# Four units of seven products in gate-and-up blocks 1 to 7, a second set of sum buffers, and low parts of four plain chunks made by accumulating GpSimd transfers

## The chip, the cores and the metric

One core of one Trainium2 chip. The metric is the device time of one execution in microseconds. A measurement is the median of several executions.

## The reference, cut to what matters

One decoder layer over 272 tokens (16 meta tokens and 256 of the input) with a model width of 2048. First a token-mixing part, which the change does not touch. Then a SwiGLU feed-forward part on the 256 tokens, with a hidden width of 5632, all in float32:

```python
u = rmsnorm(h, pre_ffn_g[i])
ff = (jax.nn.silu(u @ w_gate[i]) * (u @ w_up[i])) @ w_down[i]
h = h + rmsnorm(ff, post_ffn_g[i])
```

## The kernel before, in words

**Chunks and the ring.** All weights stream through a ring of four slots (`WSLOTS = 4`). A chunk q is 128 partitions by 1024 float32 values, 512 KB. SyncE loads it into `raw[slot]`, in gate and up as two transfers of 256 KB: 512 columns of w_gate and the same 512 columns of w_up, for one tile kt of 128 input channels. ScalarE writes its rounded high part `w_hi[slot]` (`split_hi`, L554) once the chunk has landed and TensorE has used chunk q-4. VectorE writes the low part `w_lo = raw - w_hi` (`split_lo`, L907). SyncE loads chunk q+4 into the slot once `w_lo` of chunk q is made, and, where chunk q belongs to a unit of seven products, once all sums over its raw values are made as well (L442). SyncE issues its loads strictly in order.

**Products.** The tokens stand as the transposed tiles `uf` (a high and a low part), and a product of full precision is three matmuls: high by high, high by low, low by high (`three`, L1711 to L1713), each 128x128 by 512 columns. A block g of gate and up (g = 0 to 10) is 512 hidden columns, sixteen chunks, eight pairs of chunks. A plain pair (letter P) costs 2 chunks x 4 quarters x 3 = 24 matmuls. A pair under letter Z is done by a scheme with seven products instead of eight, 21 matmuls (`seven_products`): it needs four sums of the tokens' blocks (`sums_f`, made once, in block 0) and four sums of the weights' blocks, made anew for each pair. `ROUND` writes the order of the pairs of a block by hand: block 0 is `PPPPPPPP`, blocks 1 to 10 are `PPZPZPZP`.

**The weight sums.** `weight_sums` (VectorE, L1195 to L1204) makes one sum of 512 columns into `tx[0]`, then the low half of the first chunk (L1181), then `tx[1]` (L1200), then `tx[2:4]` together (L1204). ScalarE rounds them, two at a time, to `t_hi` (`weight_sums_hi`, L838), and VectorE makes `t_lo` (`weight_sums_lo`, L1211). In between VectorE makes the low part of the pair's second chunk. There is one set of buffers `tx`, `t_hi`, `t_lo` (the last lies over `tx`), and semaphore `t_used` tells that TensorE has read a sum. In a Z pair TensorE first multiplies with the chunks themselves (3, then 6 matmuls, and then both slots are free), and then with the sums (12 matmuls). It waits for `lo_done` of the second chunk after the first three.

**What else a block has.** Seven of the products of a block's Z pairs are collected in other banks than the plain ones and folded in afterwards: in the next block's chunk 1 ScalarE copies one bank (`x0_kept`, L888) and VectorE makes combinations (`fold_sums`, L1265 to L1272); in its chunk 3, when TensorE has used every chunk of the block, VectorE folds them into the quarters (L1278, L1282), ScalarE applies silu (L815, after its `w_hi` of chunk 3) and VectorE multiplies gate and up (`gated`, L1169). TensorE transposes the result before its chunk 2 (L1774); in chunk 5 ScalarE and VectorE split it into `ffn` (L819, L1174). The order of each engine's work is the order of these loops, chunk by chunk; each engine is in order. In block 0 VectorE also makes `sums_f` for the three pairs of `SEVEN_F`, at the chunks in `F_SUM_AT`.

GpSimd has no work in this part.

Of the kernel before, what the change touches and what calls it, by code (L numbers as in the profile page):

```python
# [18 lines left out]
F32 = mybir.dt.float32  # L19
# [17 lines left out]
def build_trunk(nc, x, meta, pre_mix_g, w_in, w_pool, pool_scale, w_dw, b_dw, conv_ln_g, conv_ln_b, w_pw,  # L37
# [123 lines left out]
    with ExitStack() as ctx:  # L161
# [29 lines left out]
        t_lo = sb_at("t_lo", [P, 4, DCOLS], F32R, a_xt)  # L191
        t_hi = sb_at("t_hi", [P, 4, DCOLS], F32R, a_xt + 16 * DCOLS)
        rows_u = tx[:, 0, :].rearrange("p (k t) -> p k t", k=2)
        sums_w = tx[:, 1, :].rearrange("p (s t) -> p s t", s=4)
# [3 lines left out]
        sums_f = sb_at("sums_f", [P, len(SEVEN_F), 4, 2, P], F32R, a_y)  # L198
        gated = sb_at("gated", [P, NQ, DCOLS], F32, a_y + 4 * KT * SEQ - 8 * DCOLS)
        sums_y = sb_at("sums_y", [P, max(len(SEVEN_U) - IN_U, 1), 3, 2, P], F32R, a_y)  # L200
        assert 32 * P * len(SEVEN_F) + 8 * DCOLS <= 4 * KT * SEQ and 24 * P * (len(SEVEN_U) - IN_U) <= 4 * KT * SEQ
# [108 lines left out]
        def sem(name):  # L310
# [87 lines left out]
        def _(sp_eng):  # L398
# [64 lines left out]
        def _(pool):  # L463
# [85 lines left out]
        def _(act):  # L549
            def split_hi(q, slot, turn):  # L550
                act.wait_ge(raw_landed[slot], landed(q))
                if not isinstance(q, int) or q >= WSLOTS:
                    act.wait_ge(chunks_used, q - WSLOTS + 1)
                act.activation(w_hi[:, slot, :], raw[:, slot, :], ACT.Copy).then_inc(hi_done, 1)  # L554

            def split(q):
                split_hi(q, q % WSLOTS, q // WSLOTS)
# [346 lines left out]
        def _(dve):  # L904
# [279 lines left out]
            def weight_sums(q, z):  # L1184

                at = [(q - 1) % WSLOTS, q % WSLOTS]
                b11, b12, b22 = (raw[:, at[k], j * DCOLS:(j + 1) * DCOLS] for k, j in ((0, 0), (0, 1), (1, 1)))
                for k in range(2):
                    dve.wait_ge(raw_landed[at[k]], landed(q - 1 + k))
                if z == 0:  # L1190
                    dve.wait_ge(s_lo, 2 * len(SEVEN_F))
                else:
                    dve.wait_ge(t_used, 4 * z - 3)
                    dve.wait_ge(fold_done, len(QUARTERS) * max(min(SEVENS[z][0], NFG) - 1, 0))
                dve.tensor_tensor(tx[:, 0, :], b12, b11, ALU.add).then_inc(t_made, 1)  # L1195
                first_half_lo(q - 1)
                if z:
                    dve.wait_ge(t_used, 4 * z - 2)
                dve.wait_ge(t_made, 3 * z + 1)
                dve.tensor_tensor(tx[:, 1, :], b22, tx[:, 0, :], ALU.subtract).then_inc(t_made, 1)  # L1200
                if z:
                    dve.wait_ge(t_used, 4 * z)
                dve.wait_ge(t_made, 3 * z + 2)
                dve.tensor_tensor(tx[:, 2:4, :], raw[:, at[0]:at[0] + 2, 0:DCOLS],  # L1204
                                  tx[:, 1:2, :].to_broadcast([P, 2, DCOLS]), ALU.add).then_inc(t_made, 1)

            def weight_sums_lo(z):
                dve.wait_ge(t_made, 3 * z + 3)
                for h in range(2):
                    dve.wait_ge(t_hi_done, 2 * z + h + 1)  # L1210
                    dve.tensor_tensor(t_lo[:, 2 * h:2 * h + 2, :], tx[:, 2 * h:2 * h + 2, :],  # L1211
                                      hi_view(t_hi[:, 2 * h:2 * h + 2, :]), ALU.subtract).then_inc(t_lo_done, 1)

# [81 lines left out]
            for q in range(Q_FFN + 10, END + 4):  # L1295
                if q < END:
                    g, ch, d = place_of(q)
                    z = SEVEN_NO.get((g, d))
                    if 1 <= g <= NFG and ch == 3:
                        dve.wait_ge(chunks_used, BEGIN[g])  # L1300
                        inner_product(g - 1)
                    if z is None:
                        split(q)
                    elif ch % 2:
                        weight_sums(q, z)
                        split(q)
                        weight_sums_lo(z)
# [57 lines left out]
        def _(pe):  # L1365
# [357 lines left out]
            def plain_products(q, quarters):  # L1723
                g, ch, d = place_of(q)
                kt, chs = 2 * d + ch % 2, 2 * len(ROUND[g])
                pe.wait_ge(lo_done, q + 1)
                if g >= NFG:
                    pe.wait_ge(f_lo, kt // 4 + 1)
                for m, j in quarters:
                    if g == 0:  # L1730
# [4 lines left out]
            def seven_products(q):  # L1735
# [110 lines left out]
```

## Time and profile before

| | |
|---|---|
| time, median of 3 runs | 1076.89 us (1075.95 to 1077.07) |
| the profiled execution: its own time | 1076.7 us |
| its span | 1074.8 us |
| granted TensorE clock, mean of the span | 0.998 |

The profile is of one execution. Its rows are in microseconds from the span's start, unless they say ns. A row of the timeline gives the start, the length, the engine, the line of the kernel, the operation, output<-input, and how long the engine sat idle before it and what ended that. Neighbouring instructions of one engine overlap a little at their ends, so the distance of two starts is less than the length shown. Matmuls overlap far more: each row is about 0.39 us long, though the next begins 0.23 us after it.

### The profile page before, as it was taken

The numbers are of one execution on the slowest core, as the hardware profiler recorded it, in microseconds if no ns is written. First come the engines' busy times: TensorE is split into PE (matmuls) and PEld (weight loads), VectorE is DVE, ScalarE is ACT, GpSimd is POOL, SyncE is SP. The second block draws the span as 40 slices with busy tenths as digits, with TensorE's granted clock in tenths as the row PEclk, the third lists the DMA queues.
The fourth block names the chain that finished last, engine by engine and source line by source line (L and its number), as shares of the span: only waits on it lengthen the run. The fifth ranks groups of instructions, "written<-read, shape, count | busy, mean of one in ns | idle before, by whom it ended". The sixth has DMA issues, their size and how long they took to land. (4 is left out here: it accounts for less than half of the span.)

```text
span 1074.8 us, 15382 instructions
## 1 busy us (share of the span) xinstructions
PE 1064.1 (99%) x5745; PEld 922.1 (86%) x5745; DVE 891.3 (83%) x1083; ACT 599.2 (56%) x736; POOL 27.3 (3%) x46
## 2 busy tenths in 40 slices
PE   9999999999999999999999999999999999999996
PEld 8999999999888888888888888888888888888885
DVE  5699987646646787898998998988989899988887
ACT  6554454736545565555565655655655555655553
POOL 4000101101000000000000000000000000000000
PEclk9999999999999999999999999999999999999999
DMA  8655535444386476766756656657667655566665
GB/s 273 208 176 167 172 106 160 136 143 138 111 309 213 141 263 186 225 188 191 225 174 195 216 182 210 201 178 229 186 190 219 226 197 196 194 209 219 200 202 191
DMA packets 113208, 208.06 MB, mean 194 GB/s; under 512 B 9184, under 2 KB 46496, under 8 KB 111856
## 3 DMA queue, kind: packets, MB, share of 16 engines
q1 hardware_dynamic: 111952, 201.49, 58.6%
q10 hardware_dynamic: 608, 4.20, 1.0%
q0 software_dynamic: 576, 1.40, 0.4%
q8 instruction: 46, 0.75, 0.3%
q14 instruction: 26, 0.21, 0.1%
HBM read 202.86 MB, written 4.19 MB: 193 GB/s over the span
## 5 line engine op out<-in xcount | busy, mean ns | idle before, releaser
L554 ACT ACTIVATE w_hi<-raw 128x1024 fp32r<-128x1024 f32 x322 | 337.9, 1059 | 260.4 <-PE ps L1713 149.6
L907 DVE TENSOR_TENSOR w_lo<-raw,w_hi 128x1024 fp32r<-128x1024 f32 x322 | 390.4, 1226 | 82.5 <-ACT w_hi L554 81.9
L1711 PE MATMUL ps<-w_hi,uf 128*128 128x512 f32 x524 | 205.3, 392 | 0.1
L1713 PE MATMUL ps<-w_hi,uf 128*128 128x512 f32 x524 | 204.1, 389 | 0.0
L1712 PE MATMUL ps<-w_lo,uf 128*128 128x512 f32 x524 | 203.9, 389 | 0.0
L1375 PE MATMUL ps<-u,w_hi 128*128 128x272 f32 (+1 forms) x544 | 158.8, 292 | 0.0
L1377 PE MATMUL ps<-u,w_hi 128*128 128x272 f32 (+1 forms) x544 | 155.9, 287 | 0.0
L1378 PE MATMUL ps<-u,w_lo 128*128 128x272 f32 (+1 forms) x544 | 155.7, 286 | 0.0
L838 ACT CAST t_hi<-tx 128x1024 fp32r<-128x1024 f32 x92 | 96.3, 1052 | 65.9 <-DVE tx L1200 54.6
L1713 PEld LDWEIGHTS ps<-w_hi,uf 128*128 128x128 f32 x524 | 98.4, 188 | 20.6
L1711 PEld LDWEIGHTS ps<-w_hi,uf 128*128 128x128 f32 x524 | 98.4, 188 | 20.5 <-issue 0.5
L1712 PEld LDWEIGHTS ps<-w_lo,uf 128*128 128x128 f32 x524 | 98.4, 188 | 20.0
L1211 DVE TENSOR_TENSOR t_lo<-tx,t_hi 128x1024 fp32r<-128x1024 f32 x92 | 108.2, 1218 | 0.0
L1375 PEld LDWEIGHTS ps<-u,w_hi 128*128 128x128 f32 x544 | 102.4, 188 | 0.4
L1377 PEld LDWEIGHTS ps<-u,w_hi 128*128 128x128 f32 x544 | 102.5, 188 | 0.2
L1378 PEld LDWEIGHTS ps<-u,w_lo 128*128 128x128 f32 x544 | 102.6, 189 | 0.0
L1711 PE MATMUL ps<-w_hi,ffn 128*128 128x512 f32 x256 | 99.7, 389 | 0.0
L1713 PE MATMUL ps<-w_hi,ffn 128*128 128x512 f32 x256 | 99.6, 389 | 0.0
L1712 PE MATMUL ps<-w_lo,ffn 128*128 128x512 f32 x256 | 99.6, 389 | 0.0
L1204 DVE TENSOR_TENSOR tx<-raw,tx 128x1024 f32<-128x1024 f32 x46 | 56.4, 1225 | 4.7
L1711 PEld LDWEIGHTS ps<-w_hi,ffn 128*128 128x128 f32 x256 | 48.1, 188 | 10.0
L1712 PEld LDWEIGHTS ps<-w_lo,ffn 128*128 128x128 f32 x256 | 48.1, 188 | 10.0
(271 smaller groups left out, 1469.7 us busy)
## 6 DMA issues: line engine op xcount, KB each, us to landing
raw<-in_w_gate SPq DMA_DIRECT2D x176, 256.0 KB, 2.9
raw<-in_w_up SPq DMA_DIRECT2D x176, 256.0 KB, 3.5
raw<-in_w_down SPq DMA_DIRECT2D x88, 512.0 KB, 4.2
raw<-in_w_in SPq DMA_DIRECT2D x72, 512.0 KB, 3.6
raw<-in_w_out SPq DMA_DIRECT2D x32, 512.0 KB, 4.4
arena<-in_x SPq DMA_DIRECT2D x2, 1024.0 KB, 5.9
arena<-in_x ACTq DMA_DIRECT2D x2, 1024.0 KB, 8.5
out<-h2rows SPq DMA_DIRECT2D x2, 1024.0 KB, 5.5
```

The lines of the kernel that those rows point to most:

```text
L554: act.activation(w_hi[:, slot, :], raw[:, slot, :], ACT.Copy).then_inc(hi_done, 1)
L838: act.copy(t_hi[:, 2 * h:2 * h + 2, :], tx[:, 2 * h:2 * h + 2, :]).then_inc(t_hi_done, 1)
L907: dve.tensor_tensor(w_lo[:, slot, :], raw[:, slot, :], hi_view(w_hi[:, slot, :]), ALU.subtract).then_inc(lo_done, 1)
L1204: dve.tensor_tensor(tx[:, 2:4, :], raw[:, at[0]:at[0] + 2, 0:DCOLS], tx[:, 1:2, :].to_broadcast([P, 2, DCOLS]), ALU.add).then_inc(t_made, 1)
L1211: dve.tensor_tensor(t_lo[:, 2 * h:2 * h + 2, :], tx[:, 2 * h:2 * h + 2, :], hi_view(t_hi[:, 2 * h:2 * h + 2, :]), ALU.subtract).then_inc(t ...
L1375: pe.matmul(outs[m], w_hi[:, slot, at], x_hi, start=start and not (one_bank and m), stop=False, skip_group_check=True)
L1377: pe.matmul(outs[m], w_hi[:, slot, at], x_lo, start=False, stop=False, skip_group_check=True)
L1378: mm = pe.matmul(outs[m], w_lo[:, slot, at], x_hi, start=False, stop=last and k == len(kts) - 1, skip_group_check=True)
L1711: pe.matmul(o, a[0], b[0], start=start, stop=False)
L1712: pe.matmul(o, a[0], b[1], start=False, stop=False)
L1713: return pe.matmul(o, a[1], b[0], start=False, stop=stop)
```

## The change

In blocks 1 to 7 the order of pairs becomes `PPZZPZZP`, with four Z pairs; blocks 8 to 10 keep three. A fourth pair of token sums is made in block 0. In these blocks the Z pairs alternate between the old set of sum buffers and a second one, which lies in a part of `ffn` that is written from block 8 on (`gated` moves there too). For chunks 1, 2, 8 and 15 of these blocks VectorE no longer makes `w_lo`: ScalarE writes minus the high part into `w_lo` with one more pass over the raw chunk, right after its high part, and GpSimd issues a transfer that adds `raw` onto it in SBUF. TensorE does the eight matmuls of such a chunk that need the high part alone first, then waits for the transfer, then does the four with the low part. SyncE's load of chunk q+4 waits for the transfer as well.

```diff
-    SEVEN_F, SEVEN_U = (0, 1, 2), (11, 12, 13, 14, 15, 16, 17, 18, 19)
+    SEVEN_F, SEVEN_U = (0, 1, 2, 3), (11, 12, 13, 14, 15, 16, 17, 18, 19)
...
-    F_SUM_AT = {10: 0, 12: 1, 14: 2}
-    ROUND = ["PPPPPPPP"] + ["PPZPZPZP"] * (NFG - 1) + ["PPPPZPPZPPZPPZPZPZPZPP", "PPPZPZPZPZPZPZPZPZPZPP"]
+    F_SUM_AT = {10: 0, 12: 1, 13: 2, 14: 3}
+    WITH_SPARE = range(1, 8)
+    ADDED_CH = (1, 2, 8, 15)
+    ROUND = ["PPPPPPPP"] + ["PPZZPZZP" if g in WITH_SPARE else "PPZPZPZP" for g in range(1, NFG)] + ["PPPPZPPZPPZPPZPZPZPZPP", "PPPZPZPZPZPZPZPZPZPZPP"]
...
+    ADDED = [BEGIN[g] + ch for g in WITH_SPARE for ch in ADDED_CH]
+    ADDED_NO = {q: i for i, q in enumerate(ADDED)}
...
+    def buffers_of(z):
+
+        g, d = SEVENS[z]
+        return (z - SEVENS_TO[g - 1]) % 2 if g in WITH_SPARE else 0
...
-                sp_eng.wait_ge(lo_done, q - WSLOTS + 1)
+                if q - WSLOTS in ADDED_NO:
+                    sp_eng.wait_ge(lo_added[q % WSLOTS], lo_by_dma(q - WSLOTS))
+                else:
+                    sp_eng.wait_ge(lo_done, lo_by_dve(q - WSLOTS))
...
+            for i, q in enumerate(ADDED):
+                slot = q % WSLOTS
+                pool.wait_ge(neg_done, i + 1)
+                pool.dma_start(w_lo[:, slot, :].bitcast(F32), raw[:, slot, :], accum_op=ALU.add).then_inc(lo_added[slot], 16)
...
+            def minus_hi(q):
+                slot = q % WSLOTS
+                act.activation(w_lo[:, slot, :], raw[:, slot, :], ACT.Copy, scale=-1.0).then_inc(neg_done, 1)
...
                         split(q)
+                        if q in ADDED_NO:
+                            minus_hi(q)
                         if z is not None:
                             weight_sums_hi(z)
...
-                    if z is None:
+                    if z is None and q not in ADDED_NO:
                         split(q)
...
+                if q in ADDED_NO:
+                    pe.wait_ge(hi_done, q + 1)
+                    for m, j in quarters:
+                        for h in range(2):
+                            pe.matmul(quarter(g, m, j), left(g, kt, m)[h], right(q, j)[0], start=ch == 0 and h == 0, stop=False)
+                    pe.wait_ge(lo_added[q % WSLOTS], lo_by_dma(q))
+                    for m, j in quarters:
+                        mm = pe.matmul(quarter(g, m, j), left(g, kt, m)[0], right(q, j)[1], start=False, stop=ch == chs - 1)
+                    return mm
```

`lo_by_dve(q)` and `lo_by_dma(q)` count the low parts that each of the two makers has finished. In `weight_sums` the waits for `t_used` now name the Z pair that last used the same set of buffers.

## Rows read from the trace of the kernel before

**Rows 1.** Page, part 1: busy us (share), x instructions; then all PE waits over 0.1 us

```profile
PE 1064.1 (99%) x5745; PEld 922.1 (86%) x5745; DVE 891.3 (83%) x1083; ACT 599.2 (56%) x736; POOL 27.3 (3%) x46
...
PE ps L1417 <- POOL cst L467: 1.2, 1, 1.2
PE ps L1485 <- DVE u L928: 0.5, 1, 0.5
```

**Rows 2.** Busy time by engine in one block, 455.00 to 497.40

```profile
core 0: us, PE busy (x) PEld busy (x) DVE busy (x) ACT busy (x) POOL busy (x), PEclk, DMA share, GB/s
455.00:497.40 42.40, 42.40 (x193) 35.18 (x192) 38.59 (x40) 24.11 (x26) 0.00 (x0) 1.00 0.64 199
```

**Rows 3.** Timeline, TensorE, block 2: transposes, chunk 2, unit of seven, next pair

```profile
460.41 1.04 PE L1774 MATMUL ps<-cst,gated 128*128 128x128 f32 x8
...
461.98 0.40 PE L1711 MATMUL ps<-w_hi,uf 128*128 128x512 f32 x1
...
468.13 0.39 PE L1711 MATMUL ps<-w_hi,sums_f 128*128 128x512 f32 x1
...
471.53 0.39 PE L1711 MATMUL ps<-w_hi,uf 128*128 128x512 f32 x1
```

**Rows 4.** Timeline, VectorE, same block and `gated` of the next

```profile
457.89 1.41 DVE L1169 SCALAR_TENSOR_TENSOR gated<-ps,cst,gated 128x512 f32<-128x512 f32 x2 [0.20 <-DVE ps L1282]
...
468.03 2.35 DVE L907 TENSOR_TENSOR w_lo<-raw,w_hi 128x1024 fp32r<-128x1024 f32 x2
470.29 0.68 DVE L1195 TENSOR_TENSOR tx<-raw 128x512 f32<-128x512 f32 x1
...
472.29 1.23 DVE L1204 TENSOR_TENSOR tx<-raw,tx 128x1024 f32<-128x1024 f32 x1
473.43 1.22 DVE L907 TENSOR_TENSOR w_lo<-raw,w_hi 128x1024 fp32r<-128x1024 f32 x1
...
476.84 1.22 DVE L907 TENSOR_TENSOR w_lo<-raw,w_hi 128x1024 fp32r<-128x1024 f32 x1
...
500.30 1.41 DVE L1169 SCALAR_TENSOR_TENSOR gated<-ps,cst,gated 128x512 f32<-128x512 f32 x2 [0.20 <-DVE ps L1282]
```

**Rows 5.** Timeline, ScalarE, same block

```profile
456.19 1.25 ACT L815 ACTIVATE gated<-ps,cst 128x512 f32<-128x512 f32 x2
...
473.55 1.05 ACT L838 CAST t_hi<-tx 128x1024 fp32r<-128x1024 f32 x1 [0.28 <-DVE tx L1204]
474.51 1.06 ACT L554 ACTIVATE w_hi<-raw 128x1024 fp32r<-128x1024 f32 x1
```

**Rows 6.** DMA issues: KB each, median us from issue to landing

```profile
raw<-in_w_up SPq DMA_DIRECT2D x176, 256.0 KB, 3.5
...
out<-f_acc SPq DMA_DIRECT2D x3, 512.0 KB, 2.7
side<-in_w_pw POOLq DMA_DIRECT2D x1, 1024.0 KB, 7.7
...
side<-in_w_pool POOLq DMA_DIRECT2D x1, 256.0 KB, 4.4
```

**Rows 7.** Timeline, GpSimd: issue of the 256 KB; then DMA queues, 10 to 22

```profile
11.58 1.21 POOL L505 DMA_DIRECT2D side<-in_w_pool  x1
...
DMA  9999999999999999997478999999999995487996
```

**Rows 8.** Timeline, SyncE's queue, two loads of one block

```profile
473.59 0.33 SPq L445 DMA_DIRECT2D raw<-in_w_gate  x1
...
475.05 0.43 SPq L445 DMA_DIRECT2D raw<-in_w_up  x1
```

**Rows 9.** Timeline, VectorE, end of block 0: low parts and the idle time before them

```profile
408.50 1.23 DVE L907 TENSOR_TENSOR w_lo<-raw,w_hi 128x1024 fp32r<-128x1024 f32 x1 [1.12 <-ACT w_hi L554]
411.22 1.23 DVE L907 TENSOR_TENSOR w_lo<-raw,w_hi 128x1024 fp32r<-128x1024 f32 x1 [1.49 <-ACT w_hi L554]
416.00 1.41 DVE L1169 SCALAR_TENSOR_TENSOR gated<-ps,cst,gated 128x512 f32<-128x512 f32 x2 [3.55 <-ACT gated L815]
```

More of the change, by code:

```diff
@@ L153, in place_of, with lo_by_dve, lo_by_dma, before_in_buffers @@
         return g, ch, TURNS[g][ch // 2]
+    ADDED = [BEGIN[g] + ch for g in WITH_SPARE for ch in ADDED_CH]
+    ADDED_NO = {q: i for i, q in enumerate(ADDED)}
+    def lo_by_dve(q):
+        return q + 1 - sum(1 for a in ADDED if a <= q)
+    def lo_by_dma(q):
+        return 16 * sum(1 for a in ADDED if a <= q and (a - q) % WSLOTS == 0)
+    def buffers_of(z):
+        g, d = SEVENS[z]
+        return (z - SEVENS_TO[g - 1]) % 2 if g in WITH_SPARE else 0
+    def before_in_buffers(z):
+        return max((y for y in range(z) if buffers_of(y) == buffers_of(z)), default=None)
     def landed(q):
@@ L192, in build_trunk @@
         t_hi = sb_at("t_hi", [P, 4, DCOLS], F32R, a_xt + 16 * DCOLS)
+        a_spare = top[0] + 4 * KT * SEQ + 4 * 1152 + 4 * 4 * (max(WITH_SPARE) + 1) * 2 * SEQ
+        tx2 = sb_at("tx2", [P, 4, DCOLS], F32, a_spare)
+        t_lo2 = sb_at("t_lo2", [P, 4, DCOLS], F32R, a_spare)
+        t_hi2 = sb_at("t_hi2", [P, 4, DCOLS], F32R, a_spare + 16 * DCOLS)
+        sums_of, hi_of, lo_of = (tx, tx2), (t_hi, t_hi2), (t_lo, t_lo2)
         rows_u = tx[:, 0, :].rearrange("p (k t) -> p k t", k=2)
@@ L198, in build_trunk @@
         sums_f = sb_at("sums_f", [P, len(SEVEN_F), 4, 2, P], F32R, a_y)
[L199 removed]
+        gated = sb_at("gated", [P, NQ, DCOLS], F32, a_spare + 32 * DCOLS)
         sums_y = sb_at("sums_y", [P, max(len(SEVEN_U) - IN_U, 1), 3, 2, P], F32R, a_y)
[L201 removed]
+        assert 32 * P * len(SEVEN_F) <= 4 * KT * SEQ and 24 * P * (len(SEVEN_U) - IN_U) <= 4 * KT * SEQ
         side = sb_at("side", [P, KT * SEQ], F32, a_y)
@@ L206, in build_trunk @@
         a_ff = place(4 * FT * 2 * SEQ)
+        assert a_spare == a_ff + 4 * 32 * 2 * SEQ and 32 * DCOLS + 8 * DCOLS <= 4 * 12 * 2 * SEQ
         ffn = sb_at("ffn", [P, FT, 2, SEQ], F32R, a_ff)
@@ L347, in build_trunk @@
             sem(n) for n in ("rows_done", "turned", "h2_hi", "h2_lo", "h2_sq", "r2c_done"))
+        neg_done, lo_added = sem("neg_done"), [sem(f"lo_added{s}") for s in range(WSLOTS)]
         silu_done, p_done, f_hi, f_lo = (sem(n) for n in ("silu_done", "p_done", "f_hi", "f_lo"))
@@ L1189, in weight_sums @@
                     dve.wait_ge(raw_landed[at[k]], landed(q - 1 + k))
+                sums, y = sums_of[buffers_of(z)], before_in_buffers(z)
                 if z == 0:
                     dve.wait_ge(s_lo, 2 * len(SEVEN_F))
-                else:
-                    dve.wait_ge(t_used, 4 * z - 3)
+                if y is not None:
+                    dve.wait_ge(t_used, 4 * y + 1)
+                if y is not None and buffers_of(z) == 0:
                     dve.wait_ge(fold_done, len(QUARTERS) * max(min(SEVENS[z][0], NFG) - 1, 0))
-                dve.tensor_tensor(tx[:, 0, :], b12, b11, ALU.add).then_inc(t_made, 1)
+                dve.tensor_tensor(sums[:, 0, :], b12, b11, ALU.add).then_inc(t_made, 1)
                 first_half_lo(q - 1)
-                if z:
-                    dve.wait_ge(t_used, 4 * z - 2)
+                if y is not None:
+                    dve.wait_ge(t_used, 4 * y + 2)
                 dve.wait_ge(t_made, 3 * z + 1)
-                dve.tensor_tensor(tx[:, 1, :], b22, tx[:, 0, :], ALU.subtract).then_inc(t_made, 1)
-                if z:
-                    dve.wait_ge(t_used, 4 * z)
+                dve.tensor_tensor(sums[:, 1, :], b22, sums[:, 0, :], ALU.subtract).then_inc(t_made, 1)
+                if y is not None:
+                    dve.wait_ge(t_used, 4 * y + 4)
                 dve.wait_ge(t_made, 3 * z + 2)
-                dve.tensor_tensor(tx[:, 2:4, :], raw[:, at[0]:at[0] + 2, 0:DCOLS],
-                                  tx[:, 1:2, :].to_broadcast([P, 2, DCOLS]), ALU.add).then_inc(t_made, 1)
+                dve.tensor_tensor(sums[:, 2:4, :], raw[:, at[0]:at[0] + 2, 0:DCOLS],
+                                  sums[:, 1:2, :].to_broadcast([P, 2, DCOLS]), ALU.add).then_inc(t_made, 1)
             def weight_sums_lo(z):
+                b = buffers_of(z)
                 dve.wait_ge(t_made, 3 * z + 3)
@@ L1301, in _ @@
                         inner_product(g - 1)
-                    if z is None:
+                    if z is None and q not in ADDED_NO:
                         split(q)
-                    elif ch % 2:
+                    elif z is not None and ch % 2:
                         weight_sums(q, z)
```

15 lines of the change are left out of this document (8 added, 7 removed).

## The prediction

> **What bounds the kernel now.** I read the page's busy shares and TensorE's waits first: TensorE is busy for 99% of the span and waited 1.2 us once and 0.5 us once, never in gate and up [rows 1]. So fewer matmuls are time, as long as nothing makes TensorE wait. Then one block: from one `gated` to the next is 500.30 - 457.89 = 42.41 us [rows 4], in which VectorE is busy for 38.59, ScalarE for 24.11, GpSimd never, and the DMA engines for 0.64 [rows 2]. VectorE is the engine with no room, so what matters next is when each of its results is due.
>
> **Clock of a block.** Between two plain products 42 matmuls apart lie 471.53 - 461.98 = 9.55 us, 0.227 us each; the transposes put chunk 2 back by about 0.9 us (they start at 460.41, and the matmul at 461.98 is the fourth of that chunk, so the first stands for 461.30) [rows 3]. Chunks 0 and 1 are 24 matmuls, 5.44 us, so the block begins at 460.41 - 5.44 = 454.97; I call this 0. Check: 183 matmuls x 0.2268 + 0.9 = 42.4.
>
> **The gain.** A fourth Z pair takes 24 - 21 = 3 matmuls out of a block: 0.68 us. In seven blocks 21 matmuls, 4.8 us, if nothing waits.
>
> **VectorE's load.** A Z pair costs it 476.84 - 470.29 = 6.55 us, two low parts 470.29 - 468.03 = 2.26 [rows 4]. A fourth Z adds 4.3, four low parts less take off 4.5: even. ScalarE gets, per block, four more passes of about 1 us and one more Z (two sums of 1.05, and a half pass for a whole one): some 6 us on 24 of 42; room as a sum, but it is in order.
>
> **Where results are late: the second Z of a row.** VectorE's second Z in a row (pair 3) takes the place of the low parts at 468.03, so all of that unit moves 2.26 us earlier. Its second chunk's low part, which ended at 473.43 + 1.22 = 474.65, ends at 472.39. TensorE wants it three matmuls after pair 3 begins: 471.53 + 0.68 = 472.21. With the handoff I price this stall at 0.3 us; the sums behind it are just in time. Nothing earlier can help, because VectorE's `inner_product` starts only when the block before is used up. The same place at pair 6 has its slack back, as TensorE has a plain pair before both.
>
> **Where results are late: chunk 8.** ScalarE cannot touch chunk 8 before it has rounded the sums of pair 3. Its row at 473.55 moves to 471.29, the high part at 474.51 to 472.25 [rows 5], the new pass minus-high follows 0.96 later and ends at 474.27, which is 19.3. TensorE begins pair 4 at 471.53 + 21 x 0.227 = 476.29 and, after eight matmuls with the high part, wants the low part at 478.1. So the transfer, from GpSimd's wait to its landing, has about 4 us. Call it L. After it come 4 + 12 + 21 + 21 + 24 = 82 matmuls, 18.6 us, to the block's end. With 0.1 for handoffs a block takes 38.0 + L, or 42.0 (41.7 by the matmuls and 0.3) where L is under 4. Break-even with 42.4 is at L = 4.4. Chunks 1, 2 and 15 by the same working have over 5 us.
>
> **What L is.** No row shows an accumulating transfer, nor one from SBUF to SBUF. Nearest are two transfers that GpSimd issued: 256 KB landed after 4.4 us and 1024 KB after 7.7 [rows 6], 1.2 us of it the issue, in a stretch with the DMA engines 99% busy [rows 7]; between them 512 KB is 5.5. From below: 512 KB out of SBUF on SyncE's queue took 2.7 [rows 6], and with 1.2 for the issue 3.9. From above: the adding reads its destination too. Reading 512 KB more at (7.7 - 4.4)/768 us per KB gives 5.5 + 2.2 = 7.7. A quieter stretch takes off, a second read puts on; I take 5.2, near the one row pair that went through the same issuer, and keep 3.9 to 7.7 for the range. The Trainium skill, "Collectives: The Full Stack", on why ReduceScatter is half of AllGather, says that an add in the DMA engines needs two source reads and halves the rate; no row here shows it. By the block's own rate it would make a sum of L that is 0.64 x 42.4/16 = 1.7 us longer than a copy's.
>
> **What late adding does next.** SyncE's load of the next block's chunk 3 waits for chunk 15's transfer, and ScalarE's silu stands behind the high part of that chunk 3. Pair 6 needs chunks 12 and 13, which load behind chunk 8's transfer: a landing is 3.5 [rows 6], the second chunk's issue about 0.8 behind [rows 8], so VectorE begins pair 6 at 19.3 + L + 4.3; the last sums are rounded and ScalarE is at chunk 14 4.2 us later (470.29 to 474.51 [rows 4, 5]), three passes more end at 30.8 + L, the transfer at 30.8 + 2L, the load at 34.3 + 2L. That is L - 3.7 after the next block's start; a high part (1.06, overlapping) and the first silu (half of 1.25) [rows 5] end at L - 2.0, while `gated` starts at 2.9 today [rows 4]. So above L = 4.9 each us is paid a second time: at 5.2 it is 0.3. Block time 38.0 + 5.2 + 0.3 = 43.5, +1.1 us, in seven blocks +7.7.
>
> **At nothing.** The fourth token sum (about 2.4 us of VectorE) falls in the end of block 0, where VectorE idles 1.12, 1.49 and 3.55 us waiting for ScalarE [rows 9]; without that cover it would cost its 2.4 once. The second buffer set removes the `t_used` waits between neighbouring Z pairs; `gated`'s new place has no user before block 8. GpSimd's queue holds nothing else here, so what waits behind an add is only the next add. Stages outside blocks 1 to 7 stay.
>
> **Sum.** The profiled execution is 1076.7 us, its span 1074.8; the median is 1076.9, 0.2 above. 1076.9 + 7.7 = 1084.6.
>
> **Rivals.** (a) *The add is quick, the change pays.* L of 4.1 or less, near the lower bound: 41.7 + 0.3 = 42.0 per block, -0.4 x 7 = -3, 1073.9; for it: a plain SBUF read of this size takes 2.7, and the engines are a third idle; against it: both GpSimd rows are over 4.4. The Trainium skill, "DMA: Bandwidth & Descriptors", in the anatomy of a DMA on the GpSimd path, fits 2.0 us plus bytes/436e3: 3.2 us for 512 KB, which would bring this case about; its 4.4 for 1 MB stands against this trace's 7.7, so the trace does not agree, though in a crowded stretch. Chance 0.25. (b) *Even.* L of 4.1 to 4.7: gain and stalls cancel, 1075 to 1079. Chance 0.18. (c) *Chunk 8 is late*, the forecast: L of 4.7 to 6.5, that is +0.3 to +3.7 per block, 1079 to 1103. Chance 0.44. (d) *The DMA engines become the bound.* 512 KB costs the sixteen engines 1.7 us by the block's rate; four adds are 7 us as copies and 14 with a second read, on top of 27 of 42: a share of 0.80 to 0.96, loads land late, L is 7 to 8: 38 + 7 + 2.1 = 47.1, +33 us or more, 1110 to 1124. For it: 0.64 today [rows 2]; against it: the gaps between loads are long. Chance 0.13.
>
> **How the numbers follow.** About 0.2% (2.2 us) is what a measurement of this kernel can tell. Faster is (a), 0.25 (38.0 + 4.1 is 0.3 per block under today's 42.4); same is (b), 0.18; slower is (c) and (d), 0.57. The range runs from (a) at 1073.3 to L = 6.5 at 1103, leaving out (d) and a little below. The forecast's own range is 1079 to 1103.
>
> **What would show it.** 21 matmuls less, 28 + 7 = 35 whole low parts fewer at VectorE's L907 (a Z pair has a half for one of its two), 28 transfers on GpSimd's queue. Right: TensorE rows with idle time ended by a DMA on `w_lo`, in chunk 8 of each block, of 1 to 2 us; small idle times at pair 3 ended by VectorE's L907; loads of chunk 12 issued later. A landing time of the adding transfers under 4.1 makes the forecast wrong at that step; waits of TensorE at chunks 1, 2 or 15, or at `w_hi`, would make it wrong in place.

## The result, and the profile after

The changed kernel takes 1131.44 us (median of 5 runs, 1129.66 to 1132.93), 54.5 us more than the 1076.89 before: ratio 1.0509, 95% interval 1.0497 to 1.0521. The forecast had the sign, but 7.7 us; the measured time lies far above its range.

The page of the changed kernel: busy times; the granted clock and DMA share in 40 slices; two of its queues.

```profile
PE 1073.4 (95%) x5724; PEld 914.9 (81%) x5724; DVE 891.2 (79%) x1096; ACT 634.4 (56%) x779; POOL 51.4 (5%) x74
...
PEclk9999999999999999999999999999999999999999
DMA  8655454424685776867768676776675656566665
...
q1 hardware_dynamic: 111952, 201.49, 55.6%
q0 software_dynamic: 4608, 16.08, 7.2%
```

The matmuls went from 5745 to 5724, the 21 promised; VectorE's work is the same (891.2 against 891.3 [rows 1]), and ScalarE, with its 35 us more, is busy for the same 56%. The granted clock is at the upper level, 2.4 GHz, in all of blocks 1 to 7 but one stretch: behind TensorE's wait of 2.48 us for `gated` it fell, to a mean of 0.57 from 520 to 524, so mostly to the lower level, 1.2 GHz. Over the 49.8 us from 517.4 to 567.2 the mean is 0.97. As an estimate, the length times what the mean lacks to 1.00 is what the clock cost, 1.5 us here; I use this estimate below as well. So the loss is waiting, nearly all of it. From one `gated` to the next, the kernel before took 41.9 to 42.8 us. In the changed kernel the seven intervals that belong to blocks 1 to 7 take 50.9, 51.3, 49.8, 51.6, 49.2, 50.8 and 49.5 us, and the blocks after them 41.6, 42.4 and 42.4 again. So the loss is 8 us a block.

One block, 460.40 to 510.85 (length, busy times by engine, granted clock, DMA share, GB/s, as in [rows 2]), and then the largest waits that the change made or enlarged (total us, times, longest; the first three rows are of ScalarE and VectorE, the others of TensorE):

```profile
460.40:510.85 50.45, 43.67 (x190) 34.07 (x189) 38.31 (x41) 29.13 (x33) 3.41 (x4) 1.00 0.74 209
```

```profile
ACT w_hi L590 <- DMA raw<-in_w_up: 92.9, 50, 3.7
...
DVE tx L1240 <- issue: 28.1, 15, 2.6
...
DVE gated L1212 <- ACT gated L855: 25.7, 8, 6.4
...
PE ps L1757 <- DVE w_lo L950: 17.5, 16, 1.7
...
PE ps L1781 <- DMA w_lo<-raw: 11.4, 14, 1.3
...
PE ps L1829 <- DVE gated L1212: 10.5, 6, 2.5
...
PE ps L1757 <- DVE ffn L1217: 6.3, 6, 1.1
```

```profile
SPq L477 <- DMA w_lo<-raw: 124.9, 28, 6.7
```

Where [rows 2] had TensorE busy for all of the block, it is now idle for 6.8 of 50.45 us, and VectorE, the engine that had no room, idles 12. (Most of what 6.8 leaves of the loss stands in TensorE's busy time, 43.67 us for 190 matmuls where 193 took 42.40: a matmul's row is 0.39 us long though the next begins after 0.23, and the row behind a wait is longer.) TensorE's waits in blocks 1 to 7 are 17.5 us for VectorE's low parts (L950), 11.4 for the transfers (L1781), 10.5 for `gated` and 6.3 that end with VectorE's `ffn`. So the transfers themselves are a quarter of them; the rest is VectorE being late. The largest row is ScalarE waiting for raw chunks to land, 92.9 us against 18.9 in the kernel before. SyncE's queue waits for the adding transfers 28 times, 124.9 us in all. Its total wait at that line is what it was before (117.8 and 124.9 now, 243.7 then); what is new is when the loads go. The transfers and the loads:

```profile
raw<-in_w_gate SPq DMA_DIRECT2D x176, 256.0 KB, 3.5
raw<-in_w_up SPq DMA_DIRECT2D x176, 256.0 KB, 4.1
...
w_lo<-raw POOLq DMA_DIRECT2D x28, 512.0 KB, 6.2
```

```profile
DMA to landing us min/median/max: 5.0/6.2/7.8
```

L, from issue to landing, was 6.2 us where I took 5.2 between 3.9 and 7.7 [rows 6]; the issue is 0.86 of it. The loads' medians are 3.5 and 4.1 us, 0.6 more than the 2.9 and 3.5 before. Here is one held load after another (timelines of GpSimd, SyncE's queue, ScalarE and VectorE around the start of the block that begins at 460.4):

```profile
453.00 0.85 POOL L575 DMA_DIRECT2D w_lo<-raw  x1 [18.09 <-ACT w_lo L594]
457.08 0.85 POOL L575 DMA_DIRECT2D w_lo<-raw  x1 [3.23 <-ACT w_lo L594]
```

```profile
459.29 0.33 SPq L477 DMA_DIRECT2D raw<-in_w_gate  x1
...
463.60 1.58 SPq L477 DMA_DIRECT2D raw<-in_w_up  x1
```

```profile
464.49 1.06 ACT L590 ACTIVATE w_hi<-raw 128x1024 fp32r<-128x1024 f32 x1 [2.74 <-DMA raw<-in_w_up]
465.45 1.25 ACT L855 ACTIVATE gated<-ps,cst 128x512 f32<-128x512 f32 x2
```

```profile
466.15 1.41 DVE L1212 SCALAR_TENSOR_TENSOR gated<-ps,cst,gated 128x512 f32<-128x512 f32 x2 [3.08 <-ACT gated L855]
...
470.36 0.69 DVE L1240 TENSOR_TENSOR tx<-raw 128x512 f32<-128x512 f32 x1 [1.66 <-issue]
```

Chunk 15's transfer, issued at 453.00, lets the load of the next chunk 3 go at 459.29; that chunk is rounded at 464.49, silu follows and `gated` starts at 466.15, 5.7 us into the block instead of 2.9. Chunk 1's transfer, issued at 457.08, lets the load of chunk 5 go, its second half at 463.60; it lands at 470.3, and only then can VectorE begin the sums of pair 2, at 10.0 us into the block instead of 5.4, as this row of the kernel before shows:

```profile
460.35 0.69 DVE L1195 TENSOR_TENSOR tx<-raw 128x512 f32<-128x512 f32 x1
```

Everything behind it is late by that: chunk 8's transfer is issued at 24.1 us into the block, where I had 19.3.

The first of the seven blocks shows what a held load does by itself, as no transfer of an earlier block disturbs its start. TensorE's transposes of blocks 1 and 2, and VectorE's first sum of pair 2 in block 1, in the changed kernel:

```profile
417.29 1.04 PE L1829 MATMUL ps<-cst,gated 128*128 128x128 f32 x8
...
467.62 1.09 PE L1829 MATMUL ps<-cst,gated 128*128 128x128 f32 x8 [1.63 <-DVE gated L1212]
```

```profile
420.02 0.69 DVE L1240 TENSOR_TENSOR tx<-raw 128x512 f32<-128x512 f32 x1 [2.25 <-issue]
```

Block 1 begins 5.44 us before its transposes, at 411.85, so the sum begins at 8.2 us into the block; in the kernel before it is 5.9 (418.46, with the transposes at 418.04). The load of chunk 5 had gone out at 416.18, when chunk 1's transfer, issued at 409.79, was done. And from transposes to transposes this first block takes 50.3 us already, the next one 51.3.

### The profile page after: what moved, and what is told of

It is laid out like the page before. It is cut to its first block and busy times, and to the rows that moved or that the text cites. A ratio compares the mean times of both kernels' runs of the same rounds, so it can differ in the third digit from the quotient of the medians.

```text
span 1129.4 us, 15468 instructions
## 1 busy us (share of the span) xinstructions
PE 1073.4 (95%) x5724; PEld 914.9 (81%) x5724; DVE 891.2 (79%) x1096; ACT 634.4 (56%) x779; POOL 51.4 (5%) x74
## 5 line engine op out<-in xcount | busy, mean ns | idle before, releaser
L590 ACT ACTIVATE w_hi<-raw 128x1024 fp32r<-128x1024 f32 x315 | 330.0, 1058 | 259.7 <-DMA raw<-in_w_up 92.9
L950 DVE TENSOR_TENSOR w_lo<-raw,w_hi 128x1024 fp32r<-128x1024 f32 x287 | 349.5, 1226 | 80.8 <-ACT w_hi L590 80.2
L1757 PE MATMUL ps<-w_hi,uf 128*128 128x512 f32 x370 | 146.9, 397 | 17.7 <-DVE w_lo L950 17.5
L879 ACT CAST t_hi<-tx 128x1024 fp32r<-128x1024 f32 x106 | 110.8, 1050 | 81.3 <-DVE tx L1245 67.7
L1759 PE MATMUL ps<-w_hi,uf 128*128 128x512 f32 x370 | 144.3, 390 | 0.0
L1758 PE MATMUL ps<-w_lo,uf 128*128 128x512 f32 x370 | 144.2, 390 | 0.0
L1257 DVE TENSOR_TENSOR t_lo<-tx,t_hi 128x1024 fp32r<-128x1024 f32 x106 | 124.7, 1218 | 0.0
L1757 PEld LDWEIGHTS ps<-w_hi,uf 128*128 128x128 f32 x370 | 69.4, 188 | 39.9 <-DVE w_lo L950 25.1
L1759 PEld LDWEIGHTS ps<-w_hi,uf 128*128 128x128 f32 x370 | 69.5, 188 | 14.7
L1758 PEld LDWEIGHTS ps<-w_lo,uf 128*128 128x128 f32 x370 | 69.5, 188 | 13.6
L1249 DVE TENSOR_TENSOR tx<-raw,tx 128x1024 f32<-128x1024 f32 x53 | 64.9, 1225 | 5.8 <-DVE tx L1245 0.5
L1240 DVE TENSOR_TENSOR tx<-raw 128x512 f32<-128x512 f32 x53 | 36.5, 688 | 38.3 <-issue 28.1
L1778 PE MATMUL ps<-w_hi,uf 128*128 128x512 f32 x224 | 57.4, 399 | 0.0
```

Of the source, the lines that this page charges most:

```text
L879: act.copy(hi_of[b][:, 2 * h:2 * h + 2, :], sums_of[b][:, 2 * h:2 * h + 2, :]).then_inc(t_hi_done, 1)
L950: dve.tensor_tensor(w_lo[:, slot, :], raw[:, slot, :], hi_view(w_hi[:, slot, :]), ALU.subtract).then_inc(lo_done, 1)
L1249: dve.tensor_tensor(sums[:, 2:4, :], raw[:, at[0]:at[0] + 2, 0:DCOLS], sums[:, 1:2, :].to_broadcast([P, 2, DCOLS]), ALU.add).then_inc(t_ma ...
L1257: dve.tensor_tensor(lo_of[b][:, 2 * h:2 * h + 2, :], sums_of[b][:, 2 * h:2 * h + 2, :], hi_view(hi_of[b][:, 2 * h:2 * h + 2, :]), ALU.subt ...
L1757: pe.matmul(o, a[0], b[0], start=start, stop=False)
L1758: pe.matmul(o, a[0], b[1], start=False, stop=False)
```

## The experiments

Each is a change of the changed kernel, and its blocks are told by the distance from one `gated` to the next (kernel before: 42.4). In the fences of experiments the line numbers are of their own kernels. The first question was what the seven neighbouring pairs cost without any transfer.

**Four units of seven, no transfers.**

```diff
-    ADDED_CH = (1, 2, 8, 15)
+    ADDED_CH = ()
```

> Four units of seven in blocks 1 to 7 with both sets of sum buffers, but no transfers: VectorE makes all low parts. Theory A (the adding transfers hold the ring: SyncE's load of chunk q+4 waits for the transfer of chunk q, and such waits chain through a block): most of the 54.5 us go; what is left is VectorE's own excess, 38.6 + 4.3 = 42.9 us of work and some 2 us of gaps against 41.7 of matmuls, +1 to +3.5 us per block, 1084 to 1101. Rival B (the neighbouring units of seven are too late by themselves, transfers or not): 1120 or more.

1085.17 us, ratio 1.0084 (1.0067 to 1.0101); blocks 43.3 to 44.1. TensorE has two waits per block, at pairs 3 and 6:

```profile
517.33 0.50 PE L1757 MATMUL ps<-w_hi,uf 128*128 128x512 f32 x1 [0.61 <-DVE w_lo L950]
532.96 0.50 PE L1757 MATMUL ps<-w_hi,uf 128*128 128x512 f32 x1 [0.33 <-DVE w_lo L950]
```

So the transfers cost 46 of the 54.5 us, and the pairs themselves about 9. Rival B falls.

**The transfers with the old order of pairs.**

```diff
-    SEVEN_F, SEVEN_U = (0, 1, 2, 3), ...
+    SEVEN_F, SEVEN_U = (0, 1, 2), ...
-    F_SUM_AT = {10: 0, 12: 1, 13: 2, 14: 3}
+    F_SUM_AT = {10: 0, 12: 1, 14: 2}
-    ADDED_CH = (1, 2, 8, 15)
+    ADDED_CH = (1, 2, 10, 15)
-    ... ["PPZZPZZP" if g in WITH_SPARE else "PPZPZPZP" for g in range(1, NFG)] ...
+    ... ["PPZPZPZP"] * (NFG - 1) ...
```

> The order of pairs, the token sums and the number of units of seven as in the kernel before; chunks 1, 2, 10 and 15 of blocks 1 to 7 have their low parts added by transfers, and VectorE has 4.5 us less to do per block. Theory A: the chained waits are there though VectorE has room, 3 to 7 us per block, 1098 to 1126. Rival B: with room on VectorE nothing is late, 1075 to 1082.

1103.91 us, ratio 1.0259 (1.0241 to 1.0276), blocks 44.0 to 49.5. TensorE hardly waits for a low part here (1.1 us in all), yet the kernel loses 27 us:

```profile
ACT w_hi L590 <- DMA raw<-in_w_up: 85.4, 46, 7.9
...
PE ps L1829 <- DVE gated L1212: 12.8, 6, 4.3
...
PE ps L1781 <- DMA w_lo<-raw: 1.1, 3, 0.4
```

The transfers do harm even where VectorE has 4.5 us of room more, and they landed in 5.3 us at the median here, nearly the 5.2 that I had forecast. ScalarE's long waits for raw chunks point at late loads. A small part is the clock's: behind two waits of 4.1 and 4.3 us for `gated` the granted clock was 0.93 and 0.96 over the block, by my estimate 5 us in all.

**Adding from HBM, so that raw is free earlier.**

```diff
-                    sp_eng.wait_ge(lo_added[q % WSLOTS], lo_by_dma(q - WSLOTS))
+                    sp_eng.wait_ge(neg_done, ADDED_NO[q - WSLOTS] + 1)
...
-                pool.dma_start(w_lo[:, slot, :].bitcast(F32), raw[:, slot, :], accum_op=ALU.add).then_inc(lo_added[slot], 16)
+                g, ch, d = place_of(q)
+                for j, src in enumerate((wg_v, wu_v)):
+                    pool.dma_start(w_lo[:, slot, j * DCOLS:(j + 1) * DCOLS], src[:, 2 * d + ch % 2, g * DCOLS:(g + 1) * DCOLS], accum_op=ALU.add).then_inc(lo_added[slot], 16)
```

> As the changed kernel, but the adding transfer reads the weights from HBM again (two of 256 KB per chunk), so raw is free once ScalarE has made both of its passes, and SyncE waits for that instead of the transfer. Theory A: the chain between transfer and load is cut, only TensorE's own waits for the low parts of chunk 8 and its like stay: +1 to +4 us per block, 1085 to 1105. Rival C (the transfers slow the loads by sharing the sixteen engines; who waits for them does not matter): the HBM traffic rises further, 1125 or more.

1147.67 us, ratio 1.0654 (1.0637 to 1.0672), a miss of theory A's range; it lies in rival C's. ScalarE's waits for raw did fall (26.7 us instead of 92.9), and the loads landed in 3.6 and 4.4 us, about as in the changed kernel (3.6 and 4.3), so what rival C names is not seen. But the second of the two transfers landed after 9.0 us and TensorE waited for it 45.3 us; behind such waits the granted clock fell, to 0.91 over three of the seven blocks and 0.97 over the other four, by my estimate 21 us in all. Held slots were exchanged for longer transfers, so this run tells nothing apart.

**A copying transfer.** The low parts of the four chunks are raw values here.

```diff
-                pool.dma_start(w_lo[:, slot, :].bitcast(F32), raw[:, slot, :], accum_op=ALU.add)...
+                pool.dma_start(w_lo[:, slot, :].bitcast(F32), raw[:, slot, :])...
```

> As the changed kernel, but the transfer copies raw onto the low part instead of adding it (the low parts are then wrong by the high part). If the second read of the add is what makes it long, the landing falls from 6.2 us to about 4.5 and the time to 1095 to 1115; if the path of issue and descriptors is, the landing stays near 6 and the time within 8 us of 1131.

1096.64 us (one run), blocks 44.2 to 46.0, landing 4.2 us. DMA queue 0 in the stretch 460 to 760, of the changed kernel and then of this one (packets, MB, share of sixteen engines):

```profile
q0 software_dynamic: 3286, 11.95, 21.2%
```

```profile
q0 software_dynamic: 3297, 12.00, 11.9%
```

The same bytes take 1.8 times the engines' time when they are added; for one chunk of 512 KB (23 fall in the stretch) 2.8 us of all sixteen engines for an add and 1.6 for a copy. Of the 54.5 us, 35 hang on the add being slower than a copy. The Trainium skill, "Collectives: The Full Stack", in "Why ReduceScatter is half of AllGather", says of the add there that it needs two source reads and halves the rate; 1.8 times here is near that. But at L = 4.2 my formula 38.0 + L gives 42.2 per block, and the blocks took 45.3 on average. So the length of L is not the only error.

**Own raw buffers in blocks 1 to 3.** The ring no longer holds the four chunks there.

```diff
+    OWN = [q for q in ADDED if q < BEGIN[4]]
...
+        raw_own = sb_at("raw_own", [P, len(ADDED_CH), CE], F32, a_spare - 4 * 16 * 2 * SEQ)
+        def raw_of(q):
+            if q in OWN:
+                return raw_own[:, ADDED_CH.index(q - BEGIN[place_of(q)[0]]), :]
+            return raw[:, q % WSLOTS, :]
...
+                r = q - WSLOTS
+                if q in OWN:
+                    r = None if q - KT not in OWN else q - KT
+                elif r in OWN:
+                    r = r - WSLOTS
```

> As the changed kernel, but in blocks 1 to 3 the raw values of chunks 1, 2, 8 and 15 have buffers of their own, outside the ring, so no load of another chunk waits for an adding transfer; blocks 4 to 7 are as in the changed kernel. The transfers are the same in number, size and place. Theory A (the loads that wait for transfers are the cost): the distance from one block's gated to the next falls from 50.4 us to 43 to 46 in blocks 1 to 3 and stays in blocks 4 to 7; 1108 to 1120 in all. Rival C (the transfers cost through the DMA engines, or through TensorE's own waits for low parts): no block under 49, 1126 or more.

1123.37 us, ratio 1.0446 (1.0412 to 1.0479), between the ranges of theory A and rival C. Blocks 1 to 3: 48.2, 48.9, 45.2; blocks 4 to 7: 51.5, 49.2, 50.4, 49.0. Less of a gain than theory A said: the held slots are gone, and another wait has grown, as the adding transfers now take 7.8 us (10 of them) where the ring's took 6.2:

```profile
488.68 2.07 PE L1810 MATMUL ps<-w_lo,uf 128*128 128x512 f32 x4 [3.94 <-DMA w_lo<-raw_own]
```

This wait has a second price. A stretch behind it, then block 2 and block 3 whole (length, busy times, granted clock, DMA share, GB/s):

```profile
488.00:494.00 6.00, 5.32 (x13) 4.16 (x14) 4.84 (x6) 0.62 (x1) 0.00 (x0) 0.50 0.50 173
...
464.02:512.88 48.86, 44.84 (x189) 36.34 (x188) 38.39 (x41) 29.09 (x32) 3.42 (x4) 0.93 0.77 222
512.88:558.12 45.24, 42.39 (x189) 34.38 (x188) 38.22 (x42) 29.09 (x32) 3.43 (x4) 1.00 0.76 215
```

In blocks 1 and 2 TensorE waited 3.38 and 3.94 us for chunk 8's transfer, and the granted clock then fell to 0.50, the lower level, 1.2 GHz; in block 3 it waited 2.84 us, and the clock stayed at 1.00. A mean of 0.93 over 48 us is by my estimate 3.4 us of time. Without it the three blocks would be at about 45, inside theory A's 43 to 46.

**Adding transfers for nobody,** onto the kernel before's order of pairs and low parts.

```diff
...
+            for i, q in enumerate([BEGIN[g] + ch for g in WITH_SPARE for ch in (1, 2, 8, 15)]):
+                pool.wait_ge(hi_done, q + 1)
+                if i:
+                    pool.wait_ge(spare_added, 16 * i)
+                pool.dma_start(spare[:, :], spare_src[:, :], accum_op=ALU.add).then_inc(spare_added, 16)
```

> The order of pairs and the low parts as in the kernel before, and besides 28 adding transfers of 512 KB from SBUF to SBUF in blocks 1 to 7, at the same chunks, that nobody waits for (they add unused memory onto unused memory). Theory A: traffic alone costs little, the loads have slack: 0 to 1 us per block, 1076.5 to 1084. Rival C: the loads land too late, 1090 or more.

1076.36 us, ratio 0.9999 (0.9989 to 1.0008), although the transfers took 23.4% of the engines in 460 to 760, with a share of 0.83 for all queues together, and 6.7 us each, and the loads landed in 3.6 and 4.3 us, as late as in the changed kernel. The traffic alone costs nothing: in the kernel before, the loads have slack for it. Rival C falls as a cause by itself.

**Chunk 8 alone, and all but chunk 8.** `ADDED_CH = (8,)`:

> Four units of seven, and of the transfers only that of chunk 8. By the step of the forecast that a block takes 38.0 + L with L the landing of 5.2 to 6.2 us: 43.2 to 44.2 per block, 1082 to 1090. Theory A, with the loads of chunks 12 and 13 held by the transfer and VectorE 3.4 us busier per block than in the changed kernel: 1090 to 1104.

1101.94 us, ratio 1.0234 (1.0217 to 1.0251), blocks 45.3 to 46.8. And `ADDED_CH = (1, 2, 15)`:

> As the changed kernel, but VectorE makes the low part of chunk 8; the transfers of chunks 1, 2 and 15 stay. If chunk 8 is where the time goes, as the forecast said, a block falls from 50.4 to about 43.7 (the run without transfers) and the whole to 1083 to 1090. Theory A, every held slot costs on its own: 46 to 48 per block, 1100 to 1117.

1116.47 us, ratio 1.0363 (1.0347 to 1.0379), blocks 46.1 to 51.3. Over the 1085.2 without transfers, chunk 8 alone costs 16.8 us, the other three 31.3, all four 46.3. The three that I had found harmless are the greater part.

**The same two with own raw buffers in blocks 1 to 3.** With `ADDED_CH = (1, 2, 15)`:

> Transfers that add for chunks 1, 2 and 15, VectorE makes chunk 8; in blocks 1 to 3 the three chunks have raw buffers outside the ring. TensorE wants these low parts late, so if the held slots are the whole cost of these three, blocks 1 to 3 fall from 48.8 us to 42 to 44 and blocks 4 to 7 stay at 48 to 49. If the transfers cost in another way (their landing, the shared DMA engines), blocks 1 to 3 stay over 46.

1108.27 us, ratio 1.0296 (1.028 to 1.0312). Blocks 1 to 3: 44.0, 44.9, 43.9, on average 0.5 over the same blocks without transfers; blocks 4 to 7: 50.4, 48.4, 49.4, 48.6. With the three slots held, blocks 1 to 3 took 48.6 on average. For these chunks the held slot is the cost, though their transfers now take 8.1 us, and the granted clock is 1.00 in all of the blocks compared. With `ADDED_CH = (8,)`:

> The adding transfer of chunk 8 alone, in blocks 1 to 3 with a raw buffer outside the ring. The forecast's step for chunk 8, 38.0 + L per block, holds no held slot: with L of 5.4 to 6 us it gives 43.4 to 44.0 in blocks 1 to 3. If TensorE's wait is the whole cost of chunk 8, these blocks stay at 45.5 to 46, as in the run with chunk 8 in the ring; if the held slot has a part, they fall to 43.5 to 45.

1105.73 us, ratio 1.0274 (1.0258 to 1.029), a miss in the other direction. Blocks 1 to 3 rose from 45.3, 45.4, 46.3 to 46.4, 48.2, 47.9. Chunk 8's transfer, in the two runs, in 418 to 760 with the slot held and in 420 to 540 without, and TensorE's wait for it:

```profile
w_lo<-raw POOLq DMA_DIRECT2D x7, 512.0 KB, 5.4
```

```profile
w_lo<-raw_own POOLq DMA_DIRECT2D x3, 512.0 KB, 7.9
```

```profile
529.09 1.20 PE L1781 MATMUL ps<-w_lo,uf 128*128 128x512 f32 x4 [1.50 <-DMA w_lo<-raw]
```

```profile
487.04 1.97 PE L1810 MATMUL ps<-w_lo,uf 128*128 128x512 f32 x4 [4.18 <-DMA w_lo<-raw_own]
```

A held slot also keeps a load away while the transfer runs. Without it a load goes out beside the transfer (in block 2 the transfer is issued at 478.78 and a load's halves at 480.70 and 481.07), and the transfer lands 2.5 us later at the median. TensorE's wait for it grew by 2.7 us in the blocks shown, and in block 2 its waits at pairs 3 and 6 are gone. What tips the balance is the clock behind the longer wait:

```profile
488.00:490.00 2.00, 2.00 (x6) 1.62 (x5) 2.00 (x4) 0.62 (x1) 0.00 (x0) 0.50 0.97 277
```

It was 0.96 over each of blocks 1 to 3, by my estimate 1.9 us a block, which is the whole rise, and 1.00 in the run with the slot held. So for chunk 8 a held slot and a freed one cost about the same, and the lower clock comes on top.

**Own raw buffers and a copying transfer.** All four chunks.

```diff
-                pool.dma_start(w_lo[:, slot, :].bitcast(F32), raw_of(q), accum_op=ALU.add)...
+                pool.dma_start(w_lo[:, slot, :].bitcast(F32), raw_of(q))...
```

> As the run with own raw buffers in blocks 1 to 3, with a copying transfer in place of the adding one in all of blocks 1 to 7 (low parts wrong by the high part). If the held slots and the length of the add are together the whole loss, blocks 1 to 3 take no longer than without transfers, 42.0 to 43.7 us, and blocks 4 to 7 about 45.5 as in the run that copies; 1088 to 1094 in all. If sharing the DMA engines costs by itself, blocks 1 to 3 stay over 44.5.

1096.44 us, ratio 1.0187 (1.0171 to 1.0203). Blocks 1 to 3: 44.8, 46.2, 44.4; 4 to 7: 45.0 to 45.6. The expected 42.0 to 43.7 was missed: chunk 8's transfer still kept TensorE waiting (7.3 us in four waits, 2.33 the longest) with a landing of 5.6 us, and block 2 had a granted clock of 0.96, by my estimate 1.8 us. By the mark that I had set, blocks over 44.5, sharing the DMA engines has a part of its own; without the clock's share the three blocks average 44.5, on the mark, so this run leaves it open.

**VectorE's room without transfers: GpSimd subtracts.** The low part of some chunks is a `tensor_tensor` on GpSimd; no pass for minus the high part.

```diff
-                pool.wait_ge(neg_done, i + 1)
-                pool.dma_start(w_lo[:, slot, :].bitcast(F32), raw[:, slot, :], accum_op=ALU.add).then_inc(lo_added[slot], 16)
+                pool.wait_ge(hi_done, q + 1)
+                pool.tensor_tensor(w_lo[:, slot, :], raw[:, slot, :], hi_view(w_hi[:, slot, :]), ALU.subtract).then_inc(lo_added[slot], 1)
```

With `ADDED_CH = (3,)`:

> Four units of seven and no transfers; the low part of chunk 3 of blocks 1 to 7 is made by GpSimd, by a subtraction (some 6.4 us by the rows of 128x256 at 1.6), in place of VectorE. Theory A: VectorE's lateness at pair 3 (0.6 us of TensorE in the run without transfers) goes: 1085.2 - 4 to 9 = 1076 to 1081. Rival D (GpSimd and VectorE slow each other where both read two operands from SBUF): 1085 or more.

1076.9 us, ratio 1.0005 (0.9995 to 1.0014): 8 us less than without it, and level with the kernel before. With (3, 8):

> Four units of seven, no transfers, low parts of chunks 3 and 8 of blocks 1 to 7 by GpSimd's subtraction, which took 2.4 us for a chunk in the run with chunk 3 alone. What is left of VectorE's lateness at pair 6 goes; a block comes to 41.7 to 42.0 against 42.4: 1072 to 1075. Rival D, GpSimd slowing VectorE: 1077 or more.

1081.26 us, ratio 1.0049 (1.0036 to 1.0063). With (1, 3, 8, 15):

> The same with four chunks by GpSimd, 1, 3, 8 and 15. VectorE then has some 4 us more room per block, which nobody needs if the two chunks were enough: the same as with two, 1072 to 1075. If GpSimd holds the slots too long (2.4 us instead of 1.1) or slows VectorE, above the run with two.

1088.48 us, ratio 1.0113 (1.0097 to 1.0128). More help made it slower. In the run with chunks 3 and 8, GpSimd's subtraction of chunk 8 beside VectorE's:

```profile
516.13 2.41 POOL L578 TENSOR_TENSOR w_lo<-raw,w_hi 128x1024 fp32r<-128x1024 f32 x1 [13.99 <-ACT w_hi L593]
```

```profile
515.05 4.57 DVE L1258 TENSOR_TENSOR t_lo<-tx,t_hi 128x1024 fp32r<-128x1024 f32 x2
```

Two subtractions that take 2.35 us elsewhere took 4.57: VectorE stood still for nearly as long as GpSimd worked. In the run with chunk 3 alone GpSimd works while VectorE's operands come from PSUM (`fold`, `gated`), and VectorE's rows keep their length. So the place to put such work is where VectorE reads PSUM: chunks 1, 2 and 3, whose subtractions fall beside `fold_sums` and `fold`. With (2, 3):

> Four units of seven, low parts of chunks 2 and 3 by GpSimd. In the run with chunks 3 and 8 VectorE's two-operand reads from SBUF stood still while GpSimd worked (mean of t_lo 1464 ns instead of 1218), with chunk 3 alone they did not, as VectorE then reads PSUM. Chunk 2 falls into such a stretch too, and fold starts 0.5 us earlier: 42.0 to 42.4 per block, 1073 to 1076.5. If it collides, 1078 or more.

1073.76 us, ratio 0.997 (0.996 to 0.9981). With (1, 2, 3):

> The same with chunk 1 as well: fold_sums starts earlier, 1072 to 1076; if chunk 1's subtraction meets VectorE's low parts, 1078 or more.

1072.33 us, ratio 0.9966 (0.9953 to 0.9978), blocks 41.4, 41.8, 41.9, 41.7, 41.8, 42.0 and 42.8. It beats both kernels:

```profile
457.00:499.00 42.00, 42.00 (x190) 34.68 (x190) 39.24 (x43) 25.23 (x28) 6.65 (x4) 1.00 0.63 202
```

```profile
492.33 4.77 POOL L578 TENSOR_TENSOR w_lo<-raw,w_hi 128x1024 fp32r<-128x1024 f32 x2 [34.41 <-ACT w_hi L593]
```

```profile
492.82 0.69 DVE L1312 TENSOR_TENSOR tx<-ps,tx 128x512 f32<-128x512 f32 x1 [0.93 <-ACT tx L932]
493.62 1.23 DVE L1316 TENSOR_TENSOR tx<-ps,tx 128x1024 f32<-128x1024 f32 x1
```

TensorE is busy for the whole block again. Two subtractions on GpSimd run beside VectorE's instructions, which keep their 0.69 and 1.23 us.

## Why the prediction was wrong

**The gain** was right: 21 matmuls less. The run with GpSimd on chunks 1, 2 and 3 gets 4.3 us of the 4.8. The fourth token sum, put at nothing, delayed nothing that the rows show: the first `gated` starts at 415.24, where it started at 416.00 [rows 9].

**VectorE's load and pair 3** were nearly right. Pair 3's stall was priced at 0.3 us and is 0.61 in the run without transfers, where VectorE has four low parts more to make. That pair 6 "has its slack back" was wrong there: 0.33. In the changed kernel itself the two waits are mostly 1.2 and 0.8 to 1.7 us, as the chunks come late.

**What L is**: mis-sized by 1.0 us, 6.2 against 5.2. The interpolation between two transfers that GpSimd had issued gave 5.5, and I took something off for a quieter stretch. The second read that I set against it costs 1.2 us of all sixteen engines (2.8 less 1.6), and copy against add differs in landing by 2.0 us. By my own formula 6.2 gives 38.0 + 6.2 + 1.3 = 45.5 per block and +22 us, so the size brings 14 of the 46.8 us that were missed. The formula makes 23 us of the step from 6.2 to a copy's 4.2, and the run with the copy gained 35: what the landing costs was under-priced too, since it is paid by held loads as well. And with three Z pairs L was 5.3, as forecast, and 27 us were lost all the same.

**The step that failed** is the sentence "Chunks 1, 2 and 15 by the same working have over 5 us". It asked only when TensorE wants the low part. It did not ask when the load four chunks later has to go out, though the change puts that load behind the transfer. I priced this for chunk 15 and for chunk 8 (a second payment above L = 4.9), and not for chunk 1, which holds chunk 5's load, nor for chunk 2, which holds chunk 6's. Pair 2's sums need chunk 5 at 5.4 us into the block, and it landed at 9.9; in block 1, with a clean start, the sums began at 8.2. Even as to TensorE the sentence did not hold for chunk 15: TensorE waits for that transfer in each block, 0.4 to 0.6 us. The runs bear it out: these three chunks cost 31.3 us in the ring (how much of it is chunk 15's, whose held load I had priced, was not tried), and in blocks 1 to 3 of the run where they have raw buffers of their own the blocks average 44.3, against 48.6 with the slots held and 43.7 in the run without transfers.

**Why it chains.** I took each block's start as a clean one, with the loads of its first chunks on time. In the changed kernel they are not: pair 6 is late because chunk 8's transfer holds chunks 12 and 13, and then the loads of the next chunks 1 and 2, which wait for its sums and for chunk 14, go late, so chunk 1's transfer goes late, and so on. From block to block it does not build up: the first block, whose start is clean, takes 50.3 us from transposes to transposes, and the second 51.3. So nearly all of the loss arises within one block and at its end; the division beyond that was not tried by itself. The parts (16.8 and 31.3 us) add up to 48.1 against 46.3 for the whole, so the two groups of chunks at least do not make each other much worse.

**Chunk 8** was the right place for TensorE's wait, and the slack of 4 us was right for a block that starts on time: with chunk 8 alone TensorE waited 1.50 us at a landing of 5.4. The block took 46.0 on average and not the formula's 43.9 (43.4, and 0.5 for the second payment). Pairs 3 and 6 wait for VectorE too (0.61 and 1.11 in one block of that run's timeline), and chunks 12 and 13 load only once the transfer has landed, as the forecast had said; how much each gives was not tried. That the held load could also be a help, by keeping the DMA engines clear, was in no part of the forecast. Nor was the granted clock, which falls behind some of TensorE's longer waits; it is about 1.5 of the 54.5 us here, and more in the runs with longer waits.

**The range.** Its lower end, 1073.3, does not come out of rival (a)'s own numbers, which give 1073.9; nothing hangs on it.

**Rival (d)**, the DMA engines as the bound, came nearest in size (+33 us or more, though 1131 lies above its 1110 to 1124) for a partly wrong reason. Their share in the block is 0.74 and not 0.80 to 0.96, and 28 such transfers for nobody cost nothing at a share of 0.83. What it had right is that transfers and loads lengthen each other (loads by 0.6 us, transfers by 2.5 where loads run beside them). How the 8 us of one block of the changed kernel divide between the three causes (held slots, TensorE's wait for chunk 8, VectorE's lateness) is only bounded by these runs, since cutting one enlarges another.

## What to carry to other kernels

When an engine's work on a ring buffer goes to a slower maker, price two due times: that of the reader of the result, and that of the load that waits for the buffer; the second was the dearer here. Before taking a transfer for arithmetic, look at the idle engine itself: GpSimd's subtraction took 2.4 us where the adding transfer took 6.2 and a pass of ScalarE. Put such work where the other engine reads PSUM. And when an experiment lengthens a wait of TensorE, look at the granted clock behind it before the distances are compared.

## What the runs showed that I had not expected

An adding transfer of 512 KB within SBUF took 5.0 to 7.8 us to land in the changed kernel. Its median was 6.2 there, 5.3 and 5.4 in the runs with three Z pairs and with chunk 8 alone, and up to 8.1 beside freed loads, against 4.2 for a copy; it took 1.8 times the DMA engines' time for its bytes.

Behind TensorE's waits of 3.38, 3.94 and 4.18 us for a transfer the granted clock fell to 0.50; behind one of 2.84 it stayed at 1.00, and behind waits of 2.47 and 2.48 it fell in two other traces (0.50 from 440 to 442 with chunk 8's own buffer, 0.57 from 520 to 524 in the changed kernel). So the length of the wait alone does not say whether it falls. By the estimate above, this is most of the 3 to 4 us by which the first three blocks of one run differed (48.2, 48.9 and 45.2).

GpSimd subtracts 128x1024 float32 in 2.41 us, far from the 6.4 that I worked out from a row of a smaller shape. Beside VectorE instructions with both operands in SBUF one of the two stands still (4.57 us for 2.35 of work); beside ones that read PSUM neither does. The Trainium skill, "SBUF — State Buffer", in "Who interferes with whom", says that a VectorE instruction with two SBUF inputs contends with a GpSimd instruction that reads SBUF, and one with at most one SBUF input, outside the two-port performance modes, does not; by that rule these runs agree, in both directions.
